# Attention slots of two mixers laid out by TensorE's share of products instead of by the number of steps

## What is computed

```python
qa, ka, va, ux, gbx, gcx, qn, kn, vn, gx = split_cols(hx @ w_in)
o_a = window_gqa(rope(qa), rope(ka), va, ka_c, va_c, sink)     # 8 heads, window 128 + all context
o_b = short_conv(ux, gbx, gcx, conv_w)                         # v = conv3(gcx * ux); gbx * v
o_c = neighbourhood_attn(qn, kn, vn, kn_c, vn_c, rpb)          # 8 heads, bias by position + context
y   = sum(sigmoid(gx + b_gate)_r * (o_r @ w_branch_r)) @ w_out
```

## Time and profile before

| | us |
|---|---|
| median of 3 runs | 2262.98 (2261.45 to 2268.64) |
| the profiled execution | 2259.22, its span 2257.4 |
| TensorE busy in the span | 2197.7 (97%) |
| VectorE, ScalarE, GpSimd busy | 767.2, 546.3, 50.3 |
| layer 0's mixer | about 57 to 577 |
| layer 1's mixer | about 1020 to 1330 |
| experts | from about 1360 to the end |

### The profile page before, as it was taken

The page is one execution under the profiler, slowest core; times in us unless marked ns, Lnnn a source line. Parts: engine busy times, 40 slices in busy tenths (PEclk is TensorE's granted clock), DMA queues, the critical chain, the costliest instruction groups (busy, mean ns, idle before and its releaser), DMA issues.

```text
span 2257.4 us, 54833 instructions
## 1 busy us (share of the span) xinstructions
PE 2197.7 (97%) x24306; PEld 1618.5 (72%) x24306; DVE 767.2 (34%) x1573; ACT 546.3 (24%) x1056; POOL 50.3 (2%) x63
## 2 busy tenths in 40 slices
PE   7999999999999999998999999999999999999999
PEld 4777877778688888867898996566666666666656
DVE  4465255444644233456737642000001010101012
ACT  4244344323422222224535440000000000000001
POOL 0000010000020000000001000000000000000000
PEclk8999999999999999979999989999999999999999
DMA  6333233235482333433234578999999999999993
GB/s 255 131 113 131 85 112 148 96 122 205 168 284 99 102 110 118 163 131 113 101 110 136 168 313 315 414 405 416 407 415 405 413 405 410 411 410 410 419 400 160
DMA packets 88535, 548.92 MB, mean 243 GB/s; under 512 B 10592, under 2 KB 16480, under 8 KB 28288
## 3 DMA queue, kind: packets, MB, share of 16 engines
q1 hardware_dynamic: 55232, 352.68, 40.3%
q10 hardware_dynamic: 28912, 178.14, 19.7%
q0 software_dynamic: 4176, 14.81, 2.0%
HBM read 529.08 MB, written 16.52 MB: 242 GB/s over the span
## 4 chain that ended last, share of the span: by engine, by line
PE 85%; DVE 6%; DMA 3%; ACT 3%; issue 2%; ACTq 0%; SPq 0%; DVEq 0%
PE S L1859 15%; PE O L1859 13%; PE pp L1490 9%; PE pp L1492 9%; PE pp L1491 9%; PE T L1859 8%; PE S L1490 2%; PE S L1492 2%; PE T L1492 2%; PE T L1490 2%; PE S L1491 2%; PE T L1491 2%; DVE wsp L1002 2%; PE T L1673 1%; PE O L1660 1%
## 5 line engine op out<-in xcount | busy, mean ns | idle before, releaser
L1859 PE MATMUL S<-slabs,M 128*32 128x256 f32 x7168 | 469.8, 380 | 4.7 <-DMA slabs<-in_w_moe 4.7
L1002 DVE TENSOR_TENSOR wsp<-raw,wsp 128x1024 fp32r<-128x1024 f32 (+3 forms) x248 | 263.3, 1083 | 305.2 <-ACT wsp L667 298.8
L1859 PEld LDWEIGHTS S<-slabs,M 128*32 128x32 f32 x7168 | 231.4, 110 | 161.7 <-DMA slabs<-in_w_moe 7.0
L1490 PE MATMUL pp<-hx,wsp 128*128 128x512 f32 (+1 forms) x800 | 283.3, 354 | 18.8 <-DVE M L1230 4.7
L1859 PE MATMUL O<-slabs,M 128*32 128x256 f32 x5376 | 291.5, 379 | 0.0
L1440 DVE TENSOR_TENSOR M<-M,S 128x256 f32<-128x256 f32 x56 | 23.6, 422 | 758.9 <-ACT M L952 758.9
L1492 PE MATMUL pp<-hx,wsp 128*128 128x512 f32 (+1 forms) x800 | 275.9, 345 | 0.0
L1491 PE MATMUL pp<-hx,wsp 128*128 128x512 f32 (+1 forms) x800 | 275.9, 345 | 0.0
L1859 PE MATMUL T<-slabs,M 128*32 128x256 f32 x3584 | 275.6, 380 | 0.0
L1859 PEld LDWEIGHTS O<-slabs,M 128*32 128x32 f32 x5376 | 174.7, 110 | 115.4
L667 ACT ACTIVATE wsp<-raw 128x1024 fp32r<-128x1024 f32 (+3 forms) x248 | 226.2, 936 | 108.2 <-PE T L1492 77.4
(11 more groups left out here) (251 smaller groups left out, 2262.1 us busy)
## 6 DMA issues: line engine op xcount, KB each, us to landing
slabs<-in_w_moe SPq DMA_DIRECT2D x175, 1024.0 KB, 15.8
slabs<-in_w_moe ACTq DMA_DIRECT2D x161, 1024.0 KB, 16.9
raw<-in_w_main SPq DMA_DIRECT2D x84, 1024.0 KB, 5.0
M<-in_w_main SPq DMA_DIRECT2D x25, 1024.0 KB, 9.1
slabs<-in_w_main SPq DMA_DIRECT2D x15, 1024.0 KB, 8.1
raw<-in_w_br SPq DMA_DIRECT2D x24, 512.0 KB, 3.7
xm<-in_w_main SPq DMA_DIRECT2D x8, 1024.0 KB, 4.9
raw<-in_w_dn SPq DMA_DIRECT2D x8, 768.0 KB, 4.1
```

Of the source, the lines that this page charges most:

```text
L1002: dve.tensor_tensor(wsp[:, slot, 1, 0:w], raw[:, rslot, half * w:half * w + w], wsp[:, slot, 0, 0:w], ALU.subtract).then_inc(lo_done, 1)
L1490: mm(dst, w_hi, x_hi, start=first, stop=False)
L1859: ins = mm(banks[g // 2][32 * c:32 * c + 32, 256 * (g % 2):256 * (g % 2) + 256], x(k, g), slab_e[i % RAW_E][:, 1024 * k + 256 * c:1024 * k ...
```

## The change

`spread` no longer counts steps but parts: a step is worth 24 (its 24 matmuls of 512 columns) unless a table gives it less. Each slot goes on the step in which the sum of the parts reaches its share. Nothing else changes: the order of the steps, the number of slots, and what each slot does are as before.

```diff
+STEP_PARTS = {"br": 12, "ada": 5, "ada_t": 3, "rope_q": 1}
+
+
 def spread(steps, slots):
 
-    out, done = [], 0
-    for n, st in enumerate(steps):
-        want = (n + 1) * slots // len(steps)
+    out, done, parts = [], 0, 0
+    total = sum(STEP_PARTS.get(what, 24) for what, _, _ in steps)
+    for st in steps:
+        parts += STEP_PARTS.get(st[0], 24)
+        want = parts * slots // total
         out.append((list(range(done, want)), st))
         done = want
     return out
```

## The result

The changed kernel took 2282.16 us (median of 6 runs, 2276.46 to 2284.77), the kernel before on the same chip 2265.81 (6 runs, 2251.45 to 2272.55): a ratio of 1.0066, 95% interval 1.0039 to 1.0092, so 15 us slower, between 9 and 21. The prediction was +12.7 on 2262.98, that is 2275 with a range of 2264 to 2282.

A forecast was written before the change was run, and what follows sets the result against it. TensorE was taken as the bound, busy 2197.7 of 2257.4 us, so only waits could cost. Terms 7.2 + 2.1 - 0.7 + 1.1 + 1.4 + 1.6 made +12.7 us on the 2262.98 median: 2275, range 2264 to 2282.

The forecast's parts named there:

- gc0 then ux1: Layer 0's branch A: transposes at ux1 wait for scaling queued on VectorE behind gc0's drain; 3.5 us.
- gc2, ada8, ux3: Layer 0's branch A: wait at ux3's transposes behind gc2's drain, with only ada8 between; 1.9 us.
- gb3: Layer 0's branch A: transposes at gb3 wait behind gb2's drain, with only an ada_t between; 0.9 us.
- The old 0.9 stays: Layer 0's branch A: the existing 0.9 us transpose wait remains, slot 5 still following gc3's drain and ada9's weight splits.
- The two-bank turn: Layer 0's branch A: products after gc3, qn1 and kn3 lose attention cover and wait for ScalarE's bank drain; 2.1 us.
- The clock: One fall to half rate after the 3.5 us wait at ux1, some 3.3 us long; 1.6 us lost.
- Branch C of layer 0: Old waits of 4.8 us go, new ones of 4.1 come, including two places at 1.3 each; -0.7 us.
- Layer 1: Branch C: slot 4 delays gx(1,0) through a bank, +1.1 us; slot 7 makes br(1,2)'s drain late, +1.4.
- No change to speak of: Rival: gaps at ux1 and ux3 let other engines catch up, so other waits don't come; +2.4 us, 2265; chance 0.24.
- Faster: Rival: even spacing hides slot chains under whole products, removing branch C and layer 1 bank waits; -7.7 us, 2255; chance 0.07.
- The clock rival: Clock falls at each larger gap and branch C waits reach 2.0; +17.7 us, 2281; chance 0.1, within the slower case.
- layer 1 would be unchanged: Rival: layer 1 has nothing for the change to spread, 2.5 us less; 2272; no separate chance given.

The follow-up runs named there:

- e3: Changed kernel, but on ux, gc and gb steps VectorE scales a slot's probabilities in the slot's own row, ahead of the drain; 2269.92 us, ratio 1.0015.
- e5: Changed kernel with two slots of layer 0's branch A moved, slot 0 to ux0 and slot 4 to ada_t8; 2271.96 us, ratio 1.0018.
- e1: New slot layout for branch A only, old layout for branch C, in both mixers; 2280.31 us, ratio 1.0084 to the kernel before.
- e4: The kernel before, run again with nothing edited; 2268.6 us, ratio 1.0011.
- e2: New slot layout for branch C only, old layout for branch A, in both mixers; 2264.76 us, ratio 0.9998 to the kernel before.
- e6: Changed kernel with slots 7 and 8 of layer 1's branch C put back on br(1,3) and br(1,4); 2268.85 us, ratio 1.0024.
- e8: Changed kernel with three dummy matmuls behind each modulation product of the two norm stages; 2272.17 us, ratio 1.0044 to the kernel before.
- e7: The kernel before with three dummy matmuls behind each modulation product of the two norm stages; 2262.9 us, ratio 0.9997.
- e9: The kernel before with slots 0 to 3 of layer 1's branch A moved to gc0, gc1, gc2 and gc3; 2267.96 us, ratio 0.9998.
- e10: e9 plus one dummy matmul behind each modulation product of the two norm stages; 2268.12 us, ratio 1.0001 to the kernel before.

## Why the prediction was right

Right in sign and in place, and in the mechanism of its largest term, the waits at the transposes of layer 0's branch A. The mechanism was wrong for layer 1's slot 4, and the sum came out near by terms that were off both ways. The time, 2282.16, lies at the very end of its range. On the 2265.81 of the same chip the predicted +12.7 would be 2278.5, 3.7 under what was measured. By stages, as means over all profiled executions with the one or the other layout, the change costs +10.4 in A0 (four with the new layout, 195.9 to 197.9, against 186.0), -0.7 in C0 (308.6 against 309.3, six each, with a fall of the clock in two of the new and three of the old ones, see below) and +2.6 in C1 (166.0 over five, 163.4 over six): 12.3, beside the sum of 12.7. But the falls of the clock lie unevenly in these means, in four of the six old C1s and in one of the five new ones. With 1.7 taken off for each fall the change costs +8.3 in A0, -0.4 in C0 and +3.4 in C1, 11.3 in all; by the runs it is 11.9 at full clock, and the sum without its clock term is 11.1, made up of 9.3, -0.7 and 2.5. The rest of the measured 15 is within its interval.

Point by point:

- **gc0 then ux1**: 3.5 predicted, 3.28 measured, by the chain given. Shown by e3 and e5, which take the wait away in two ways.
- **gc2, ada8, ux3**: 1.9 predicted; 1.51 and 0.22 measured, 1.73 together.
- **gb2** 0.4 and **gb3** 0.9 predicted; 0.22 and 0.86 (0.64 and 0.22) measured. **qn0**: 0.5 predicted, nothing measured.
- **The old 0.9 stays**: wrong. Slot 5 still lies behind gc3's drain and ada9's splits, but no wait stands there. The 0.9 was slot 4's wait at ada_t9, and no slot lies on ada_t9 now: the next transposes come at gb1, behind that turn. 7.2 new and 0.9 kept would be 8.1 at the transposes, and 6.1 were measured; a net rise of 5.2 where the sum had 7.2.
- **The two-bank turn**: 0.8, 0.8 and 0.5 predicted for gc3, qn1 and kn3; 0.41, 0.41 and about 0.35 measured, 1.2 in all against 2.1. The exponentials that I put ahead of the drain didn't delay it as I thought.
- **The clock**: one fall behind ux1 for 3.3 us, 1.6 lost, predicted. In this profile it fell there and nowhere else in branch A, and stood at 0.50 to about 105.3, so 1.7 were lost. Branch A's busy time grew by 3.4 in all, and for the other 1.7 I had no term; e5, without the fall, still has 185.7 against 184.6, and why is open. It makes up for much of the waits that I had too high (9.3 predicted, 6.7 more idle time measured), and so 10.9 was predicted for the stage and 10.1 measured. Part of the hit is luck.
- **Branch C of layer 0**: the old waits went, as said. Of the two new places priced at 1.3 each, br(0,7) to gx(1,0) cost nothing and br(0,1) to gx(0,2) 0.64 at the scores and 2.13 at the transposes, the latter just over the bound of 2; the other five profiles with this layout have 1.62 to 1.83 there. My bound was the longest old wait, and nearly all of this one has a cause that the longest old one (2.05) hadn't, shown below. What the change does to the stage is small all the same. With no fall of the clock in it, it takes 308.2 to 308.6 in the old layout (before, e1, e4) and 307.9 to 308.0 in the new one (e2, e3, e5, e6): -0.5 against the -0.7 predicted. Some 1.7 more come with a fall at its start, which both layouts show: the new one in its own profile and e8, the old one in e7, e9 and e10. In e9, with the old layout in layer 0, TensorE's busy time, clock and DMA there are

```profile
290.00:300.00 10.00, 10.00 (x60) 0.83 0.60 237
```
- **Layer 1**: 2.5 predicted, 3.4 measured with the falls of the clock taken off (165.4 to 166.2 against 161.7 to 162.5). Slots 7 and 8 make 1.3 to 2.1 of it by e6, where 1.4 was said. What is left in e6, slots 4 and 9, is 1.6 to 2.4, where 1.1 was said, and it comes another way. I had slot 4 delay the bank of gx(1,0). That wait is 2.03 or 2.04 in all profiles of the new layout and 1.34 to 2.33 in those of the old one, so no loss can be seen there. What is new are waits at two transposes (TensorE), for two scalings of VectorE that take 1.30 each instead of 0.49 beside GpSimd's masks:

```profile
1229.45 0.66 PE L1678 MATMUL T<-ident,M 128*128 128x128 f32 x4 [0.51 <-DVE M L1177]
1230.85 0.66 PE L1678 MATMUL T<-ident,M 128*128 128x128 f32 x4 [0.75 <-DVE M L1177]
...
1228.09 1.30 DVE L1177 TENSOR_SCALAR M<-M,st 128x512 f32<-128x512 f32 x1
1229.50 1.30 DVE L1177 TENSOR_SCALAR M<-M,st 128x512 f32<-128x512 f32 x1
...
1227.51 3.00 POOL L628 TENSOR_TENSOR M<-M,cmask 128x512 f32<-128x512 f32 x2 [16.86 <-DMA M<-in_rpb_rows]
```

All six profiles with slot 4 on gx(0,7) have the two long scalings. In the old layout e7 and e10 have them too, and TensorE waits at most 0.3, since its transposes come a step later there. So the meeting alone doesn't make the wait; whether the earlier place alone would, no run shows.

**The rivals.** No change to speak of rested on the gaps giving the other engines time to catch up. They don't: 1.2 us of new bank waits stand beside 6.1 at the transposes, and layer 1's rose. Faster failed at the point named: gc0's drain took 3.3 us where that rival left it under 0.2. The clock rival gave 2281, nearly this time, but not for its reason: its second fall, behind ux3, came in one of four profiles (e6) and not in the changed kernel's, whose second fall in the mixer, in branch C, the old layout shows as well. That layer 1 would be unchanged doesn't hold either.

**What I didn't see**: that executions of one kernel differ by 11 us in a stage that nothing touches. I read the norm stages of before only as fixed. Their clock stood in the profile, and a thin stage at 0.94 could have been a lucky one. Nor did I see that a fall of the clock behind a wait of 2 us comes in one execution and not in the next: from the earlier trace rows I took it that there is none after the gap of 288 to 290, and three of the six profiles with that very gap have one.

## What to carry to other kernels

Where one engine drains a product and also serves a chain in order, what counts for placing a piece of that chain is the drain ahead of it in its queue, not an even share of the bound engine's time: lay it behind steps whose drain is short or another engine's, or let the chain go ahead of the drain where the step is long. Work out each place from two timelines (what the bound engine still has to do, what the other has to finish), for two bad places of 19 made most of branch A's loss. Before two profiled executions are compared, profile the same kernel twice and look at each stage's clock.

## What the runs showed of the hardware

**The clock in thin stages is a matter of the execution.** The same code ran its norm stage in 26.8 us at a granted clock of 0.94 and in 36.3 at 0.67. Over the runs of the kernel before, time and mean granted clock go together (correlation -0.87 to -0.93 in its three sets), and some 41 us of its 2265 are lost to clocks below 1.00. Behind full-length products a wait of 3.28 us was followed by about 3.3 us at 0.50, in all four profiles that had the wait (changed, e1, e6, e8); without it (e3, e5) the same stretch stood at 1.00. Behind shorter waits it comes in some executions of the same code and not in others: behind the wait at transposes at the start of branch C in three of six with the old layout (e7, e9, e10; the wait is 2.04 to 2.06 in all six) and in two of six with the new one (changed 2.13, e8 1.83); behind ux3's 1.51 in one of four; behind gx(1,0) in four of six with the old layout (waits of 1.84 to 2.33; none at 1.34 and 1.93) and in one of six with the new one (2.03, as in the others).

**VectorE slows down beside GpSimd.** Slot 1's chain in branch C, VectorE's timeline in the changed kernel:

```profile
302.81 1.66 DVE L1007 TENSOR_TENSOR wsp<-raw,wsp 128x512 fp32r<-128x512 f32 x1 [1.20 <-ACT wsp L672]
304.58 1.53 DVE L1177 TENSOR_SCALAR M<-M,st 128x512 f32<-128x512 f32 x1
306.21 0.49 DVE L1177 TENSOR_SCALAR M<-M,st 128x512 f32<-128x512 f32 x1
```

and GpSimd's:

```profile
302.65 1.27 POOL L628 TENSOR_TENSOR M<-M,cmask 128x512 f32<-128x512 f32 x1 [27.56 <-DMA M<-in_rpb_rows]
304.56 1.26 POOL L628 TENSOR_TENSOR M<-M,cmask 128x512 f32<-128x512 f32 x1 [0.64 <-DMA M<-in_rpb_rows]
```

A split (the kind that takes 0.69 us elsewhere) took 1.66 beside the first mask, and a scaling took 1.53 beside the second, where the next one, with GpSimd idle, took 0.49. That is 2.0 us more on the chain. TensorE was ready for the transposes at 304.03 (306.16 less 2.13); without the two stretches the first scaling would have ended near 304.1. So nearly the whole wait of 2.13 is this meeting. No run took the masks away, but the other five profiles with this layout bear it out: there the two instructions together are 1.49 to 1.70 us longer than alone, the wait is 1.62 to 1.83, and in all six it is 0.12 or 0.13 us over that lengthening. The Trainium skill, "SBUF — State Buffer", in "Who interferes with whom", says that the two engines share a pair of ports, that a VectorE instruction with two inputs in SBUF contends with a GpSimd one that reads it, as a scalar operation can in the modes that use both ports, and that whoever issues first keeps the pair until its instruction ends. The trace agrees in both cases: each VectorE instruction started just behind a mask, and ended 0.55 and 0.29 us after it.
